# Later convolution tiles and earlier projection pieces in the mixer layers of a two-block network, with five smaller moves

## The reference

```python
y_gdn  = gdn_branch(...)    # 6 heads: depthwise convolution of 5 taps, silu, l2-normed q and k,
                            # a gated delta rule in both directions in chunks, rms_norm
y_mla  = mla_branch(...)    # 6 heads: low-rank q and kv, rotary part, softmax over 256 keys
y_rwkv = rwkv7_branch(...)  # 4 heads: token shift, learned decay, a delta-like state in both directions
mix = jnp.concatenate([y_gdn, y_mla, y_rwkv], axis=-1) * jax.nn.silu(cols['gate'])
x = x + mix @ w_out[layer]
```

## Time and profile before

| | us |
|---|---|
| median of three runs | 1279.88 |
| lowest, highest | 1277.46, 1287.02 |
| profiled execution, whole time | 1276.81 |
| profiled execution, its span | 1275.0 |
| TensorE matmuls busy | 1218.2 |
| VectorE busy | 738.6 |
| ScalarE busy | 351.4 |
| GpSimd busy | 47.0 |

### The profile page before, as it was taken

One profiled execution on the slowest core, in us unless ns is written; L12 is line 12 of the kernel. 1 busy time (PEld: TensorE's weight loads), 2 busy tenths in 40 slices (PEclk: granted clock), 3 DMA queues, 4 the chain that ended last, 5 costly groups with the idle time before them and its releaser, 6 DMA issues.

```text
span 1275.0 us, 18476 instructions
## 1 busy us (share of the span) xinstructions
PE 1218.2 (96%) x7257; PEld 878.2 (69%) x7257; DVE 738.6 (58%) x1471; ACT 351.4 (28%) x756; POOL 47.0 (4%) x92
## 2 busy tenths in 40 slices
PE   6999899999999999999999989999899999998997
PEld 5877549996446674599944468658577587576783
DVE  3254466766443135577654347884877269867782
ACT  2253411211002134112100034243443232434532
POOL 1100000000000000000000000010200000102100
PEclk9999999999999999999999999998889999999998
DMA  9732105545443433345454453130001433110000
GB/s 296 252 129 73 66 1 199 198 140 193 176 155 131 166 106 124 109 157 184 147 198 159 154 180 134 67 133 2 0 3 51 167 131 132 67 68 1 3 1 33
DMA packets 65853, 149.24 MB, mean 117 GB/s; under 512 B 2097, under 2 KB 8135, under 8 KB 65767
## 3 DMA queue, kind: packets, MB, share of 16 engines
q1 hardware_dynamic: 62432, 141.63, 31.5%
q0 software_dynamic: 1216, 3.52, 1.1%
q10 hardware_dynamic: 2119, 2.91, 0.9%
HBM read 146.95 MB, written 1.07 MB: 116 GB/s over the span
## 4 chain that ended last, share of the span: by engine, by line
PE 86%; DVE 8%; ACT 3%; issue 1%; ACTq 1%; DMA 0%; DVEq 0%; SPq 0%
PE banks L485 15%; PE banks L497 15%; PE banks L445 9%; PE banks L1211 4%; PE banks L582 4%; PE banks L564 4%; PE banks L904 4%; PE banks L567 2%; PE banks L901 2%; PE banks L434 2%; PE banks L931 2%; PE banks L454 1%; PE banks L998 1%; PE banks L832 1%; PE banks L711 1%
## 5 line engine op out<-in xcount | busy, mean ns | idle before, releaser
L1371 ACT ACTIVATE region<-banks 128x384 f32<-128x384 f32 (+8 forms) x159 | 76.9, 483 | 323.8 <-PE banks L445 105.0
L445 PE MATMUL banks<-hnT,weight_slabs 128*128 128x256 f32 x576 | 126.6, 380 | 3.4 <-DVE hnT L1869 3.4
L445 PEld LDWEIGHTS banks<-hnT,weight_slabs 128*128 128x128 f32 x576 | 108.8, 190 | 20.1 <-DVE hnT L1869 4.1
L497 PE MATMUL banks<-weight_slabs,region 128*128 128x512 f32 x256 | 115.1, 592 | 0.0
L497 PEld LDWEIGHTS banks<-weight_slabs,region 128*128 128x128 f32 x256 | 48.5, 190 | 60.3 <-issue 60.3
L497 PE MATMUL banks<-region 128*128 128x512 f32 x192 | 87.6, 592 | 0.0
L1852 DVE TENSOR_TENSOR region<-weight_slabs 128x1024 f32<-128x1024 f32 x32 | 39.2, 1225 | 80.3 <-PE banks L497 76.4
L2010 DVE TENSOR_TENSOR region<-banks,region 128x128 f32<-128x128 f32 x40 | 11.7, 292 | 117.4 <-PE banks L612 91.5
L1852 DVE TENSOR_TENSOR region<-weight_slabs,region 128x1024 f32<-128x1024 f32 x64 | 78.2, 1221 | 1.1
L1852 DVE TENSOR_TENSOR region<-region 128x256 f32<-128x256 f32 (+15 forms) x162 | 74.0, 457 | 5.5 <-DVE region L2323 0.4
L497 PEld LDWEIGHTS banks<-region 128*128 128x128 f32 x192 | 36.5, 190 | 45.9 <-issue 45.9
(11 more groups left out here) (367 smaller groups left out, 2035.0 us busy)
## 6 DMA issues: line engine op xcount, KB each, us to landing
weight_slabs<-in_mlp_w SPq DMA_DIRECT2D x32, 2048.0 KB, 8.5
weight_slabs<-in_w_in SPq DMA_DIRECT2D x10, 2048.0 KB, 7.8
weight_slabs<-in_od_w_in SPq DMA_DIRECT2D x6, 2048.0 KB, 8.0
weight_slabs<-in_ev_w_in SPq DMA_DIRECT2D x4, 2048.0 KB, 11.1
weight_slabs<-in_w_out SPq DMA_DIRECT2D x4, 2048.0 KB, 9.0
weight_slabs<-in_ev_w_out SPq DMA_DIRECT2D x2, 2048.0 KB, 8.1
weight_slabs<-in_od_w_out SPq DMA_DIRECT2D x2, 2048.0 KB, 7.9
weight_slabs<-in_w_in SPq DMA_DIRECT2D x2, 2016.0 KB, 8.1
```

What stands on the lines that cost most here:

```text
L445: ins = mm(view(ps, b + i * S, (1, S)), view(slabs, o + k * width + c0, (1, P)), view(hnT, k * S, (1, S)), start=k == 0, stop=k == KC - 1)
L497: ins = mm(view(ps, b, (1, 512)), view(R, act + k * st, (1, P)), view(w, wt + k * step_, (1, 512)), start=n == 0 and k == 0, stop=n == 7 a ...
L1371: say(A(dst, view(ps, b, *(dims or ((1, n),)), np_=np_), ACT.Copy, scale=scale), read("scalar", *key))
```

## The change

Seven edits. (1) The eight DMAs that lay out layer 0's compressed value matrix are issued by GpSimd, not by ScalarE. (2) After the second MLP, tile 0's product with the final gain (`x_gained`) is formed as soon as that tile is done; the halving of the GDN and RWKV row parameters moves behind the scaling of x in layer 2. (3) At the end, the row factor and the gain are applied in one VectorE operation for each half row, and the result leaves in four stores. (4) Fillers: three steps instead of two after each chunk matrix pair of direction 1; none at ("Y", 0) and ("Z", 0) of the RWKV inversion; one, one, two and one steps of the late gate instead of two each at ("Y", 1), ("Z", 1), ("VT", 2) and ("Z", 2), the three that are left being drained after `Ur`; the third decay group ahead of the second `Yr`. (5) Convolution: tile 4 at the place of 6, nothing at that of 7, 5 at that of 8, 6 and 7 after the inversion, 8 after the states. (6) ScalarE's Silu and square follow these, with the table loads placed anew. (7) GDN base: `rope` after row 3 in place of before row 0, one step of the late gate in place of the dummy matmul, the third score product at ("Y", 0), a gate step at ("Z", 0) for that at ("Y", 1), the rotated keys copied after the first tile's `ukv`.

```diff
@@ sync
             for t in range(T):
-                sp.wait_ge(*at("result_ready", t))
-                sp.dma_start(out[0, t * P:(t + 1) * P, :], view(hn, t * D, (1, D))).then_inc(*up("result_stored", t, by=16))
+                for half in range(2):
+                    sp.wait_ge(*at("result_ready", t, half))
+                    sp.dma_start(out[0, t * P:(t + 1) * P, 512 * half:512 * half + 512], view(hn, t * D + 512 * half, (1, 512)))\
+                        .then_inc(*up(f"result_stored_{t}_{half}", 0, by=16))
@@ tensor
-                        fill(2)
+                        fill(2 + d)
...
-                    elif (what, n) in (("Y", 0), ("Z", 0)):
-                        fill(2)
...
-                    elif (what, n) != ("Y", 2):
-                        for _ in range(2):
+                    else:
+                        for _ in range({("Y", 1): 1, ("Z", 1): 1, ("VT", 2): 2, ("Z", 2): 1}.get((what, n), 0)):
                             next(first_gate, None)
...
                         close(ins, ("cum", L))
+                        decay_group(2)
...
                     if n == 1:
-                        decay_group(2)
                         decay_group(3)
...
-                SCORES = {("base", 10): 0, ("base", 12): 1, ("Z", 0): 2, ("Z", 1): 3, ("X", 2): 4, ("U", 0): 5}
+                SCORES = {("base", 10): 0, ("base", 12): 1, ("Y", 0): 2, ("Z", 1): 3, ("X", 2): 4, ("U", 0): 5}
-                GATES = {("base", 14): 3, ("Y", 1): 1, ("VT", 2): 1, ("Y", 2): 1, ("Z", 2): 1, ("X", 2): 1}
+                GATES = {("base", -1): 1, ("base", 14): 2, ("Z", 0): 1, ("VT", 2): 1, ("Y", 2): 1, ("Z", 2): 1, ("X", 2): 1}
...
-                    if (what, n) == ("base", -1):
-                        warm(1, "five")
@@ gpsimd, after its parameter loads (removed from scalar, behind cmp_kv_ready)
+            pool.wait_ge(*at("vbd_cleared", 0))
+            pool.wait_ge(*at("cmp_kv_ready", 0))
+            for h in range(8):
+                pool.dma_start(view(R, VBD + h * 64, (1, 64), p0=16 * h, np_=15), view(R, VCN + (h // 4) * 64, (1, 64), np_=15))\
+                    .then_inc(*up("vbd_ready", 0, h, by=16))
@@ scalar
                     rstd(SS + t, 1, 1.0 / D, 0)
+                    if which == "fin":
+                        act.sem_inc(up("end_rstd_ready", t)[0], 1)
+                        continue
...
                 conv_in(2, 0, 1)
-                nc.scalar.preload_act_table_set("silu_and_others")
                 copy_out(view(R, LOW, (1, 376)), "low", L, 0, n=376)
-                act.wait_ge(*at("conv_sum_ready", L, 0))
-                step(A(view(R, GC, (1, 1536)), view(R, GC, (1, 1536)), ACT.Silu, scale=2.0))
-                say(A(view(R, GP, (1, 1536)), view(R, GC, (1, 1536)), ACT.Square), up("gdn_squares_ready", L))
...
-                nc.scalar.preload_act_table_set("natural_log_exp_and_others")
...
-                    if (what, n) == ("VT", 2):
-                        act.wait_ge(*at("conv_sum_ready", L, 1))
-                        step(A(view(R, GC + 1536, (1, 768)), view(R, GC + 1536, (1, 768)), ACT.Silu, scale=2.0))
-                        nc.scalar.preload_act_table_set("natural_log_exp_and_others")
+                    if (what, n) == ("Z", 2):
+                        act.wait_ge(*at("conv_sum_ready", L, 0))
+                        step(A(view(R, GC, (1, 1536)), view(R, GC, (1, 1536)), ACT.Silu, scale=2.0))
...
                 latents_T(1)
+                nc.scalar.preload_act_table_set("natural_log_exp_and_others")
...
                 decay(1)
+                say(A(view(R, GP, (1, 1536)), view(R, GC, (1, 1536)), ACT.Square), up("gdn_squares_ready", L))
+                nc.scalar.preload_act_table_set("silu_and_others")
+                act.wait_ge(*at("conv_sum_ready", L, 1))
+                step(A(view(R, GC + 1536, (1, 768)), view(R, GC + 1536, (1, 768)), ACT.Silu, scale=2.0))
+                nc.scalar.preload_act_table_set("natural_log_exp_and_others")
                 rwkv_rhs(1)
@@ vector
                 signal("x_updated", nxt, nL, 0, 1)
+                if L == 1:
+                    x_gained(0)
...
-                        if (d, s) == (1, 1):
-                            dve.wait_ge(*at("bank_read_by_scalar", "gqkv", L, 1, 0))
-                            conv((4, 5))
-                            signal("conv_sum_ready", L, 0)
...
                     if (what, n) == ("late", 0):
-                        dve.wait_ge(*at("bank_read_by_scalar", "gqkv", L, 1, 1))
-                        conv((6,))
+                        dve.wait_ge(*at("bank_read_by_scalar", "gqkv", L, 1, 0))
+                        conv((4,))
                     if (what, n) == ("Z", 0):
                         gate_mul(1, 0)
-                        dve.wait_ge(*at("bank_read_by_scalar", "gqkv", L, 2, 0))
-                        conv((7,))
                     if (what, n) == ("Z", 1):
-                        conv((8,))
-                        signal("conv_sum_ready", L, 1)
+                        conv((5,))
+                        signal("conv_sum_ready", L, 0)
...
                 invert(("r", L), "r", False, rwkv_between)
+                dve.wait_ge(*at("bank_read_by_scalar", "gqkv", L, 1, 1))
+                conv((6, 7))
...
+                        dve.wait_ge(*at("bank_read_by_scalar", "gqkv", L, 2, 0))
+                        conv((8,))
+                        signal("conv_sum_ready", L, 1)
...
-                        if n == -1:
+                        if n == 3:
                             rope()
...
-                dve.wait_ge(*at("hn_ready", "fin", 4, t))
+                dve.wait_ge(*at("end_rstd_ready", t))
...
-                v = view(hn, t * D, (1, D))
-                tt(v, v, view(rows, R_FIN, (1, D)), MUL)
-                signal("result_ready", t)
+                for half in range(2):
+                    say(V.scalar_tensor_tensor(view(hn, t * D + 512 * half, (1, 512)), view(x, t * D + 512 * half, (1, 512)),
+                                               view(sm, SS + t, (1, 1)), view(rows, R_FIN + 512 * half, (1, 512)), MUL, MUL),
+                        up("result_ready", t, half))
```

26 lines of the change are left out of this document (12 added, 14 removed).

## The result

The changed kernel took 1295.9 us (median of four runs, 1291.95 to 1296.73) beside 1279.13 for the kernel before on the same chip; the ratio is 1.0109, 95% interval 1.0083 to 1.0134. The profiled execution has a span of 1294.7 us, 19.7 more than before's 1275.0; the medians are 16.8 apart.

What follows compares the result with a forecast made beforehand. TensorE, working 96% of the span, was taken as the bound, with VectorE's chain becoming it in the RWKV inversion. 1275.0 - 1.6 - 2.5 - 1.5 - 1.2 + 14.4 = 1282.6 span, so median 1287.5, range 1272 to 1297.

Steps and rivals of the forecast that it cites:

- forecast case: Whole kernel: the terms add up as walked, 7 us slower (2 to 12), own range 1282 to 1292; chance 0.5.
- The clock rival: RWKV half: TensorE's clock falls in both layers behind the added idle time, +3.5 to +7, 1291 to 1294; chance 0.18.
- Value matrix, -1.6: Layer 0: with GpSimd issuing the eight DMAs, TensorE's 1.58 us wait before the first softmax exponentials goes; gain 1.6.
- Boundary, -2.5: Second MLP to layer 2: ScalarE's chain starts 4 us earlier, tile 1's transposes 2.5 us earlier; gain 2.5, bounds 1.5 and 2.5.
- Tail, -1.5: End of kernel: last half ready 0.9 us earlier, another 0.6 from a smaller last store; gain 1.5, bounds 0.5 and 2.2.
- First base row, +6.5: RWKV half: four more filler steps drawn before the base rows move the first from 1093.01 to 1099.5 us.
- Inversion 35.7 in place of 39.1: RWKV half, first base row to first `Ur`: VectorE's chain becomes the bound, 35.7 us instead of 39.1; bounds 29.9 and 39.1.
- Drained gate products, +2.65, and second decay group, +1.45: RWKV half: three leftover gate products drained behind `Ur` cost 2.65; the decay group moved ahead of second `Yr` costs 1.45.
- ScalarE's later Silu and square, zero: RWKV half, between second decay and second right sides: with two table loads they end about in time; cost zero, bound 2.
- GDN base, -0.6 a layer: GDN base: rope's and the products' new places bring VectorE's last base row 0.6 us earlier; bounds -1.5 and 2.
- The inversion hides the missing fillers: RWKV inversion: VectorE's chain shrinks to its own 29.9 us, the two layers cost nothing, 1270 to 1279; chance 0.22.
- The value matrix was not late: Layer 0 rival: the matrix lands late from GpSimd, TensorE waits at 94.66 and the 1.6 is lost, 1289; chance 0.02.

Runs made afterwards that it cites:

- run with both dummies: Changed kernel plus two dummy products at ("Y", 1) of the GDN inversion and two more at ("Y", 1) of the RWKV inversion: 1284.95 us against 1282.23, ratio 1.0023.
- RWKV half alone: Kernel before with only edits on fillers and second decay group, convolution tiles, and ScalarE's Silu and square: 1298.80 us against 1281.09, ratio 1.0141.
- fillers undone: Changed kernel with only the filler and late gate draws put back to their old places: 1280.95 us against the kernel before's 1281.09, ratio 0.9996.
- GDN base alone: Kernel before with only the GDN base edit (rope, key copies, order of score, gate and warming products): 1286.17 us against 1281.09, ratio 1.0029.
- scores and gates: Kernel before with only the GDN half's new order of score, gate and warming products, rope and key copies as before: 1292.19 us against 1281.82, ratio 1.0075.

## Why the prediction was right in kind and 8 us short

It forecast 1287.5 and got 1295.9: slower, as said, inside the wide range (1272 to 1297), above the forecast case's own range (1282 to 1292) and just outside the 1% to which it gave 0.74. The range held by 1 us, and partly by luck: what filled its upper end was half clock in the GDN half, which no case of the prediction had. The clock rival (1291 to 1294, chance 0.18) came nearer than the forecast. Step by step:

- **What bounds the kernel.** Right for the RWKV half: with the fillers back the inversion takes TensorE's 39.2 us whatever VectorE does, with the fillers gone it takes VectorE's chain. TensorE is busy 33.04 of 37.8 us there, 87%; the idle time is 4.8 us and not the 7 said, as the products run longer at half clock. The waits that were said (1 to 3 us each before Y 0, Y 1, `VT` and `Ur`) are 1.39, 2.50, none and 0.71.
- **Value matrix, -1.6.** Right; the wait of 1.58 is gone. The matrix landed in time: a DMA of these took 4.9 us (median from issue to landing), and the wait at its reader is still for ScalarE.
- **Boundary, -2.5.** 2.9 at the first projection, some 2.4 at the first chunk matrix. "Nothing waits for VectorE" did not quite hold: TensorE waits 0.70 us for it there.
- **Tail, -1.5.** 1.05 measured. The four stores took 2.84 us in issue, hardly less than the two of before (3.21), so the smaller last store brought little of the 0.6.
- **First base row, +6.5.** 6.5 measured (36.1 in place of 29.6 from the first chunk matrix).
- **Inversion 35.7 in place of 39.1.** The walk was right to 0.1 in its sum and to 0.3 in each part: 35.6 in both layers in the run with both dummies. In the changed kernel it is 37.8 and 38.0: the other 2.2 us are the half clock over ("Y", 1) and "VT", which the sum left to a rival. By parts: 16.0 to Y 0 (16.0 said), 6.7 to Y 1 (6.4), then 10.2 in layer 2 and 9.9 in layer 3 to Y 2 (8.2; 8.1 and 7.9 in the run with both dummies), and 5.2 to `Ur` (5.1).
- **Drained gate products, +2.65, and second decay group, +1.45.** 4.1 said; from `Ur` to the first up-projection a changed layer without a low stretch (the RWKV half alone) takes 33.7, the kernel before 29.8: 3.9. The decay group by itself: 31.1 less 29.8 is 1.3.
- **ScalarE's later Silu and square, zero.** Right: with all of it in place and the fillers undone, that stretch grew by 1.3 us in layer 3, which the decay group's 1.45 covers. ScalarE's timeline in the changed kernel:

```profile
1153.92 1.48 ACT L1731 ACTIVATE region<-region 128x1536 f32<-128x1536 f32 x1
1155.43 1.28 ACT L1732 ACT_TABLE_LOAD   x1
1156.72 0.84 ACT L1734 ACTIVATE region<-region 128x768 f32<-128x768 f32 x1
1157.59 1.28 ACT L1735 ACT_TABLE_LOAD   x1
1158.88 0.38 ACT L1375 ACTIVATE region<-banks 128x256 f32<-128x256 f32 x1
```

  Each switch cost its 1.28 us, with the next instruction 0.01 behind it. The 2.66 us that the Trainium skill (ScalarE: Activation LUTs, "What ACT_TABLE_LOAD costs") gives a switch are not seen here; the measurement decides.
- **GDN base, -0.6 a layer: the step that failed.** Base and level 0 did better than said: 37.9 and 36.6 in place of 39.9 and 38.8, 2.1 less, and the wait of 3.9 us that was said for the third `ukv` is 2.2. But Y 1 to last Z went from 11.7 and 11.6 to 16.6 and 16.5. So +2.8 a layer in place of -0.6, 6.8 us for both. The step counted products and waits, and moving one gate product away from ("Y", 1) leaves their count as it is. What it left out is that this product stood right ahead of the place where the kernel before gets its full clock back: its half-clock stretches end at 940.7 and 1200.1 us, and Y 1 begins at 940.7 and 1200.7.

Most of the excess is then accounted for. Said for the two layers from the chunk matrices on: 2 x (7.2 - 0.6) = 13.2. Measured: 22.2. Of the 9.0 between them, 6.8 are the GDN half, 2.2 the RWKV half (6.0 us more in layer 2, where the kernel before had a stretch of half clock too, 10.6 in layer 3, 14.4 said for both). By the spans of the profiled executions the excess is 12.1 (19.7 in place of 7.6). The other 3 us are the small parts: 4.1 was said to be saved ahead of layer 2, and its first chunk matrix starts only 1.5 earlier (797.2 in place of 798.7), 1.7 of the difference by the half clock at 32.6 us; the tail is 0.45 short.

The rivals. "The inversion hides the missing fillers" was to be decided by a first-row-to-`Ur` time below 33: it was 37.8, and 35.6 at full clock. The clock rival was right that both layers would fall in the RWKV inversion (13.7 us each), at a price of 2.2 a layer in place of up to 3.5; it said nothing of the GDN half, where the dearer stretch lay. The Trainium skill (TensorE: Matmul & The Clock Gate, "What's actually happening"), which it named, holds that activity releases the throttle; that dummy products, whose result nobody uses, took the stretch over the second level away agrees with it. The value matrix was not late.

Shown: that the filler draws carry the loss of the RWKV half (alone +22 us; undone, no more than the decay group's 1.3 us is left there in layer 3), that the order of score, gate and warming products carries that of the GDN half (9.6 us alone; undone it gives back 5.5 by the ratios, and the full shape in one layer of two), and that dummy products at ("Y", 1) of both inversions take back most of the loss, with the half-clock time down from 72 to 33 us. Not shown: why the clock falls where it does in the GDN half. Over the profiled executions, one of each kernel, of the 8 GDN inversions with no 512-column product at ("Y", 1) (the changed kernel, GDN base alone, fillers undone, scores and gates) all 8 ran from Y 1 to the last Z in 16.3 to 16.9 us; of the 20 with one, 18 did it in 11.6 to 12.3 and two in 17.3. Both exceptions have rope after row 3, but so have 10 of the 18. What sets them apart from their twin layers was not found.

## What to carry to other kernels

When work is moved away from a place, price the clock of what stands behind it too: the count of products was conserved here, and the 215 to 217 records of the second level took 16.5 us in place of 11.6. Fillers drawn ahead of a chain that another engine sets are missed inside it: 6.5 us of steps drawn earlier gave back 3.5 at best, what the chain behind them could shrink, and 1.3 with the half clock. And take a change with seven edits apart: three of these were worth 0.6% and came out beneath four that cost 1.7%.

## What the runs showed of the hardware

Half clock has no single price. It cost 2.2 us of a 13.7 us stretch in the RWKV inversion, where VectorE's chain set the pace, and 4.9 of the 10.6 to 11.0 us that lie over Y 1 to last Z, where TensorE did: a sixth or nearly half, by who is waited for. Over 166 runs of all kernels here (without the one of 3630.87 us), the span of one kernel varies with its own half-clock time at 0.32 us per us, which takes the scatter within a kernel from 3.4 us to 1.6. So most of the spread of the kernel before (1274 to 1290 us over the jobs) goes with the clock, and part of it comes early: the first chunk matrix of layer 2 lay anywhere from 794.7 to 810.9 us in the profiled executions, though little of what precedes it was changed. That the 21 us of half clock that the changed kernel has more (72 against 51) would by that rate be 6.7 us of its 14 to 17 is worked out, not shown.
